# NSA's heads in pairs on halves of the array, a ring of three score banks, and the scalings on Pool

## The chip, the core and the metric

The kernel runs on one core of one Trainium2 chip. The metric is the device time in microseconds; three runs of the kernel before took 2819.25, 2820.51 and 2828.82 us, median 2820.51. Engines: PE (TensorE), DVE (VectorE), ACT (ScalarE), POOL (GpSimd) and SP (SyncE, which issues transfers). Each has its own queue of instructions, in order; they meet through semaphores.

## The reference

One step of a decoder layer on 320 tokens: 256 of a prompt and 8 sequences of 8 new tokens, each with 256 past tokens. A SwiGLU, then a token mixing of two kinds of heads, then a second SwiGLU, each with a layer norm. The change touches only the token mixing. Cut to what matters:

```
# GLA, 4 heads (dk 128, dv 256), per chunk of 64 tokens; b = cumsum(log_a)
attn = einsum('bhik,bhijk,bhjk->bhij', qi, exp(b_i - b_j, causal), ki)
o    = einsum('bhij,bhjv->bhiv', attn, vi) + einsum('bhik,bhkv->bhiv', qi * exp(b), S)
S    = exp(b_last) * S + einsum('bhjk,bhjv->bhkv', ki * exp(b_last - b), vi)
o_g  = head_rms_norm(o_g, gla_norm_g) * silu(gr)

# NSA, 16 heads of 64 on 4 key/value heads: three softmaxes over the same queries,
o_c = cmp_attention(q, k_cmp, v_cmp)     # compressed keys, 15 of them
o_s = sel_attention(q, ...)              # selected blocks
o_w = window_attention(q, ...)           # a window of 512
o_n = g[..., 0:1] * o_c + g[..., 1:2] * o_s + g[..., 2:3] * o_w    # g: three gates per head
```

All is float32. With 256 past tokens the selected blocks cover everything, so the selected and the window branch are two causal softmaxes over the same positions with different keys and values.

## The kernel before

The program is a row of stages: first SwiGLU, projection, mixing, output projection, second SwiGLU. `mixing_stage` is written by hand: one block of instructions for each engine, with semaphores between them. After a preparation it runs a loop of slots, and the order in which each engine's block goes through a slot is the order of its queue.

*NSA.* There are 40 items: 32 heads (two key/value groups `p`, a half `a` = 0 or 1, a query `g`, and a query tile `qt` whose keys are 128 or 256 wide) and the eight sequences, put in at items 9, 13, ... 37. For item i: PE's `scores` (L1218 main, L1222 compressed; L1233, L1234, L1236 for a sequence), DVE's `item` (causal mask L1441, maxima L1453 and L1465, bias L1467), ACT's `exps` (L1637, L1639, with row sums), DVE's weights in the next slot (reciprocal L1450, gate L1463) and the three scalings of the probabilities (L1472 to L1474), PE's `turn` (transposes, L1260 and L1264), ACT's `take` (L1653, L1658), PE's `outputs` (L1277, L1279; L1289, L1291 for a sequence) and ACT's `out`. A head uses 64 rows of the array for scores (`a` chooses which) and 64 columns for outputs. The turn of an item stands LAG = 3 slots behind its scores, the outputs 4; the probabilities have a ring of four buffers, scores alternate between banks 0 and 1, outputs between 4 and 5. The past keys of a sequence are turned by `turn_keys` (L1245) and taken by ACT (L1646).

*GLA.* Eight levels, each of them also the state step of one sequence. A level takes two slots: in the first PE makes its scores (L1141, L1135) and DVE merges them (L1375); in the second PE makes the inter product (L1150) and the state product of a sequence (L1157), DVE makes the differences (L1350, L1351), the next level's q (L1357) and the state (L1384). ACT makes the decay (L1586), the keys of one sequence (`k_one`, L1591) and copies the inter bank (L1610); POOL the next level's k (L1524) and the gate's products with the norm's weights (L1553). GLA's jobs alternate between banks 6 and 7 in the order of `gjobs`: a job may start when the one before last on that list has been read.

PE's order in a slot: keys to turn, scores of item i, turn of item i-3, outputs of item i-4, GLA.

Of the kernel before, what the change touches and what calls it, by code (L numbers as in the profile page):

```python
# [34 lines left out]
P = 128  # L35
# [35 lines left out]
def constants():  # L71
# [32 lines left out]
    for b in range(NB):  # L104
        c[b * TS:(b + 1) * TS, K_SEQ + b] = 1.0
    return c
# [720 lines left out]
def mixing_stage(L, s):  # L827
# [3 lines left out]

    nc, A, O, bank, proj = L.nc, L.A, L.O, L.bank, L.proj
# [14 lines left out]
    k_tok = L.sb("k_tok", [P, 3, GH * P], scope=s)  # L847
# [4 lines left out]
    k_one = [L.sb(f"k_one{i}", [NS, GH * P], scope=s) for i in range(2)]  # L852
# [12 lines left out]
    S_cmp = [L.sb(f"scores_cmp{i}", [P, 16], scope=s) for i in range(2)]  # L865
    PR = L.sb("probs", [P, RING, 2 * GW + 16], scope=s)
    PT = [L.sb(f"probs_turned{i}", [P, 5, P], scope=s) for i in range(2)]
    stat = [L.sb(f"stat{i}", [P, 5, 3], scope=s) for i in range(RING)]
    k_cmp = L.sb("k_cmp", [P, NB + 1, 2, 16], scope=s)
    v_small = L.sb("v_small", [48, NB + 1, 256], scope=s)  # L870
# [8 lines left out]
    R = PR[:].rearrange("p i w -> p (i w)")[:, 0:2 * KV * P].rearrange("p (n k m) -> p n k m", n=2, k=KV)  # L879
    xc, xs = (x[:].rearrange("p a b -> p (a b)").rearrange("p (i t) -> p i t", i=2) for x in PT)  # L880
# [11 lines left out]
    items = [(p, a, g, qt) for qt in range(2) for p in range(2) for g in range(G) for a in range(2)]  # L892
    FIRST, EVERY = 9, 4
    for b in range(NB):
        items.insert(FIRST + EVERY * b, None)
    seq = {FIRST + EVERY * b: b for b in range(NB)}
    at_item = {b: i for i, b in seq.items()}
    NI = len(items)
    SLOTS = NI + LAG + 1
    turns = []  # L900
    for i in range(SLOTS):
        for n in range(2):
            if i + 2 - n in seq:
                turns.append(("k", seq[i + 2 - n], n))
        if LAG <= i < NI + LAG:
            turns.append(("p", i - LAG, 0))
    turn_no = {x: n for n, x in enumerate(turns)}

# [7 lines left out]
    for step in range(1, 2 * LEVELS + 1):  # L916
        if step % 2:
            gjobs += [("score", (step + 1) // 2, j) for j in range(parts((step + 1) // 2))]
        else:
            gjobs += [("inter", step // 2 - 1), ("state", step // 2 - 1, 0), ("state", step // 2 - 1, 1)]  # L920
    O_STEP = 2 * LEVELS + 1
    P_STEP, MS_STEP = O_STEP + 4, O_STEP + 5
# [7 lines left out]
    def last_score(lv):  # L930
# [3 lines left out]
    diffed, made_e, made_q, made_k, q_in, k_made, squared, rooted, o_step, o_inverse = (  # L934
        L.sem("gla_" + x) for x in ("diff", "e", "q", "k", "q_in", "k_one", "squared", "root", "o_step",
                                    "o_inverse"))
# [12 lines left out]
    scored, masked, maxed, exped, summed, weighed, turned, taken, small_taken, out_ready, out_taken = (  # L949
        L.sem("att_" + x) for x in ("scored", "masked", "maxed", "exped", "summed", "weighed", "turned",  # L950
                                    "taken", "small_taken", "out_ready", "out_taken"))

    def width(i):
        return GW if i in seq else (items[i][3] + 1) * P
# [17 lines left out]
    with nc.Block() as block:  # L972
        @block.sync
        def _(sp):
# [52 lines left out]
            for i in range(SLOTS):  # L1027
                if i >= 3 and i % 2 and (i - 3) // 2 < NB:
                    store_state((i - 3) // 2)
                if i >= 4 and i % 2 == 0 and 2 <= i // 2 < NB:  # L1030
                    load_state(i // 2)
                if i == 5:
                    sp.wait_ge(kv_stored, 16 * (6 + 2 + NB))
                    sp.wait_ge(cleared, 3)
# [10 lines left out]
                if i in seq and seq[i] + 2 < NB:  # L1045
                    b = seq[i] + 2
                    sp.wait_ge(turned, turn_no["k", b - 2, 1] + 1)
                    past(b, 0, past_k[b % 2], k_in[b % 2])
                if i - LAG - 2 in seq and seq[i - LAG - 2] + NV < NB:
                    b = seq[i - LAG - 2] + NV  # L1050
                    sp.wait_ge(out_ready, at_item[b - NV] + 1)
                    past(b, 1, past_v[b % NV], v_in[b % NV])
                if i == P_STEP + 1:
# [4 lines left out]
                if i == MS_STEP + 2:  # L1058
# [9 lines left out]
        def _(pe):  # L1068
# [76 lines left out]
            def gla_state(b):  # L1145
# [28 lines left out]
            def gla_step(g):  # L1174
                if g == 0:
# [7 lines left out]
                    gla_scores(0)  # L1183
                elif g < O_STEP and g % 2:
                    gla_scores((g + 1) // 2)
                elif g < O_STEP:
                    gla_state(g // 2 - 1)
                elif g < P_STEP:
                    for n in (2 * (g - O_STEP), 2 * (g - O_STEP) + 1):
                        gla_output(n)  # L1190
                elif g == P_STEP:
# [7 lines left out]
                elif g < MS_STEP + 2:  # L1199
                    for h in (2 * (g - MS_STEP), 2 * (g - MS_STEP) + 1):  # L1200
# [7 lines left out]
            def scores(i):  # L1208
                if i >= 2:
                    pe.wait_ge(exped, 3 * (i - 1))  # L1210
                main, small = bank[i % 2], bank[2]
                if i not in seq:
                    p, a, g, qt = items[i]
                    w = width(i)
                    r = slice(a * HD, (a + 1) * HD)
                    qT = proj[r, T_NQ + 4 * p + g, qt * P:(qt + 1) * P]
                    for n in range(2):
                        pe.matmul(main[:, n * w:(n + 1) * w], qT, proj[r, T_KV + 4 + 4 * n + p, 0:w],  # L1218
                                  start=True, stop=True)
                    if i:  # L1220
                        pe.wait_ge(masked, 2 * i)
                    pe.matmul(small[:, 32:48], qT, k_cmp[r, NB, p], start=True, stop=True).then_inc(scored, 1)  # L1222
                    return
                b = seq[i]
# [3 lines left out]
                c = TP + b * TS  # L1228
                for p in range(2):
                    o = slice(64 * p, 64 * p + 64)  # L1230
                    qT = q_s[:, p, b].rearrange("p a c -> p (a c)")
                    for n in range(2):
                        pe.matmul(main[o, n * 256:(n + 1) * 256], qT, KT[b % 2][:, n, p], start=True, stop=True)  # L1233
                        pe.matmul(small[o, 16 * n:16 * n + 16], qT, proj[:, T_KV + 4 + 4 * n + p, c - TS:c + TS],  # L1234
                                  start=True, stop=True)
                    mm = pe.matmul(small[o, 32:48], qT, k_cmp[:, b, p], start=True, stop=True)  # L1236
# [12 lines left out]
            def turn(i):  # L1249
                if turn_no["p", i, 0]:  # L1250
                    pe.wait_ge(taken, turn_no["p", i, 0])
                pe.wait_ge(weighed, i + 1)
                if i >= 2:
                    pe.wait_ge(out_taken, i - 1)
                w, x = PR[:, i % RING], bank[4 + i % 2]
                chunks = min(width(i), PAST) // P
                for n in range(2):
                    at = WIN + 16 if n and i in seq else n * WIN
                    for g in range(chunks):
                        pe.transpose(bank[3][:, (chunks * n + g) * P:(chunks * n + g + 1) * P],  # L1260
                                     w[:, at + g * P:at + (g + 1) * P], ident)
                if i in seq:
                    pe.transpose(x[0:32, 2 * P:3 * P], w[:, NEW:NEW + 32], ident)
                pe.transpose(x[0:16, P:2 * P], w[:, CMP:CMP + 16], ident).then_inc(turned, 1)  # L1264

            def outputs(i):
                pe.wait_ge(small_taken, i + 1)
                pt, x = PT[i % 2], bank[4 + i % 2]
                if i not in seq:
                    p, a, g, qt = items[i]  # L1270
                    kv = 2 * p + a
                    o = x[a * HD:(a + 1) * HD, 0:P]
                    chunks = width(i) // P
                    for n in range(2):
                        for c in range(chunks):
                            at = (3 + 2 * n) * 256 + kv * HD
                            pe.matmul(o, L.kv_tok[:, c, at:at + HD], pt[:, chunks * n + c],  # L1277
                                      start=(n == 0 and c == 0), stop=False)
# [589 lines left out]
```

## Time and profile before

| | |
|---|---|
| median of three runs | 2820.51 us |
| profiled execution | 2824.61 us |
| its span in the profile | 2822.4 us |
| mean granted clock of PE | 0.958 |
| PE busy in the span | 2718.7 us, 96% |
| DVE, ACT, POOL busy | 1563.6, 460.6, 762.9 us |

What is predicted is the median; the parts are read from the one profiled execution. A row of windows gives for a stretch of the span the busy time of each engine and, as PEclk, the mean clock that PE was granted, as a share of its upper level of 2.4 GHz; 0.5 is the lower level. The mixing's loop of slots lies between 1425.4 and 1684.3 us.

### The profile page before, as it was taken

Reading aid. Unit: us, or ns where it says so; the run is one execution under the profiler, and the core shown is the slowest. Engines: PE = TensorE matmul, PEld = TensorE weight load, DVE = VectorE, ACT = ScalarE, POOL = GpSimd, SP = SyncE. Lnnn points to the kernel's source line nnn. Section 1 sums busy time; section 2 is a strip of 40 time slices with the busy share of each in tenths; the row PEclk is TensorE's granted clock in tenths of the full one; section 3 lists DMA queues with packets and bytes.
Section 4 is the critical chain, followed back from the end, with each engine's and each line's share of the span. In section 5 each row is a group of like instructions: output and inputs, shape, how many; then the busy total and the mean of one; then the engine's idle time right before and its main releaser. Section 6 shows DMA issues by size and latency. Waiting matters only on the chain. (4 is left out here: it accounts for less than half of the span.)

```text
span 2822.4 us, 45319 instructions
## 1 busy us (share of the span) xinstructions
PE 2718.7 (96%) x17691; PEld 2606.0 (92%) x17691; DVE 1563.6 (55%) x1539; ACT 460.6 (16%) x1106; POOL 762.9 (27%) x564
## 2 busy tenths in 40 slices
PE   8999999999999999999799989899999999999997
PEld 7999999899999979999477769789999999999996
DVE  5555556455555665554355565565565565565555
ACT  2110001111000140000344560131100000000002
POOL 1331332133133630000211034443223313323352
PEclk9999999999999999999777999989999999999998
DMA  6555555455555435674322316435455455555552
GB/s 185 149 154 159 149 148 145 129 149 158 157 149 149 133 97 154 180 149 119 119 91 75 104 42 147 111 105 149 134 164 149 136 162 149 140 143 163 149 138 78
DMA packets 735573, 384.97 MB, mean 136 GB/s; under 512 B 65546, under 2 KB 729994, under 8 KB 735194
## 3 DMA queue, kind: packets, MB, share of 16 engines
q1 hardware_dynamic: 735386, 384.17, 49.7%
q8 instruction: 32, 0.52, 0.1%
q14 instruction: 27, 0.22, 0.0%
q10 hardware_dynamic: 128, 0.05, 0.0%
HBM read 372.24 MB, written 16.00 MB: 138 GB/s over the span
## 5 line engine op out<-in xcount | busy, mean ns | idle before, releaser
L316 PE MATMUL bank<-xh_before,wh_before 128*128 128x320 f32 x2112 | 657.6, 311 | 14.0 <-DVE wl_before L334 13.9
L317 PE MATMUL bank<-xl_before,wh_before 128*128 128x320 f32 x2112 | 656.1, 311 | 0.0
L318 PE MATMUL bank<-xh_before,wl_before 128*128 128x320 f32 x2112 | 655.8, 311 | 0.0
L316 PE MATMUL bank<-xh_after,wh_after 128*128 128x320 f32 x1664 | 521.4, 313 | 23.7 <-DVE wl_after L334 15.2
L332 DVE CAST wh_before<-raw 128x2048 fp32r<-128x2048 f32 (+1 forms) x196 | 219.9, 1122 | 579.8 <-PE bank L318 537.6
L317 PE MATMUL bank<-xl_after,wh_after 128*128 128x320 f32 x1664 | 518.4, 312 | 0.0
L318 PE MATMUL bank<-xh_after,wl_after 128*128 128x320 f32 x1664 | 518.3, 311 | 0.0
L334 DVE TENSOR_TENSOR wl_before<-raw,wh_before 128x2048 fp32r<-128x2048 f32 (+1 forms) x196 | 463.5, 2365 | 6.7
L332 DVE CAST wh_after<-raw 128x2048 fp32r<-128x2048 f32 (+1 forms) x168 | 184.9, 1101 | 437.2 <-PE bank L318 435.3
L316 PEld LDWEIGHTS bank<-xh_before,wh_before 128*128 128x128 f32 x2112 | 399.6, 189 | 15.8 <-issue 12.3
L334 DVE TENSOR_TENSOR wl_after<-raw,wh_after 128x2048 fp32r<-128x2048 f32 (+1 forms) x168 | 409.5, 2438 | 5.8
L317 PEld LDWEIGHTS bank<-xl_before,wh_before 128*128 128x128 f32 x2112 | 399.5, 189 | 0.4 <-issue 0.4
L318 PEld LDWEIGHTS bank<-xh_before,wl_before 128*128 128x128 f32 x2112 | 399.6, 189 | 0.0
L552 POOL TENSOR_TENSOR proj<-proj 128x320 f32<-128x320 f32 x88 | 126.5, 1438 | 893.8 <-ACT proj L537 893.8
L316 PEld LDWEIGHTS bank<-xh_after,wh_after 128*128 128x128 f32 x1664 | 315.5, 190 | 29.5 <-DVE wl_after L334 15.8
L317 PEld LDWEIGHTS bank<-xl_after,wh_after 128*128 128x128 f32 x1664 | 316.3, 190 | 0.0
L318 PEld LDWEIGHTS bank<-xh_after,wl_after 128*128 128x128 f32 x1664 | 316.1, 190 | 0.0
L316 PE MATMUL bank<-ffn_hh,wh_after 128*128 128x320 f32 x704 | 217.9, 310 | 0.9 <-POOL ffn_hl L557 0.9
L316 PE MATMUL bank<-ffn_hh,wh_before 128*128 128x320 f32 x704 | 217.9, 309 | 0.0
L318 PE MATMUL bank<-ffn_hh,wl_before 128*128 128x320 f32 x704 | 217.5, 309 | 0.0
L317 PE MATMUL bank<-ffn_hl,wh_after 128*128 128x320 f32 x704 | 217.5, 309 | 0.0
L317 PE MATMUL bank<-ffn_hl,wh_before 128*128 128x320 f32 x704 | 217.5, 309 | 0.0
(239 smaller groups left out, 3253.2 us busy)
## 6 DMA issues: line engine op xcount, KB each, us to landing
raw<-in_w_ffn_in SPq DMA_DIRECT2D x176, 1024.0 KB, 5.6
raw<-in_w_ffn_out SPq DMA_DIRECT2D x128, 704.0 KB, 4.9
raw<-in_w_in SPq DMA_DIRECT2D x36, 1024.0 KB, 5.5
raw<-in_w_in SPq DMA_DIRECT2D x16, 512.0 KB, 5.2
raw<-in_w_out SPq DMA_DIRECT2D x16, 512.0 KB, 4.4
raw<-in_w_out SPq DMA_DIRECT2D x64, 128.0 KB, 4.2
proj<-in_cache_cmp_kv SPq DMA_DIRECT2D x64, 64.0 KB, 2.4
raw<-in_state_gla SPq DMA_DIRECT2D x8, 512.0 KB, 3.5
```

What stands on the lines that cost most here:

```text
L316: pe.matmul(out, L.wh[a][:, w], hi[:, k], start=(k == 0), stop=False)
L317: pe.matmul(out, L.wh[a][:, w], lo[:, k], start=False, stop=False)
L318: last = pe.matmul(out, L.wl[a][:, w], hi[:, k], start=False, stop=(k == nk - 1))
L332: dve.tensor_copy(L.wh[a][:, 0:n], L.raw[a][:, 0:n]).then_inc(L.hi[a], 1)
L334: dve.tensor_tensor(L.wl[a][:, 0:n], L.raw[a][:, 0:n], L.wh[a][:, 0:n].bitcast(F32), ALU.subtract).then_inc(L.split[a], 1)
L552: pool.tensor_tensor(hid, gate, up, ALU.mult).then_inc(product, 1)
```

## The change

*Units.* The 40 items become 24 units: eight pairs (`a` = 0 and 1 together) of width 128, then eight times a sequence and a pair of width 256. There are 25 slots; a unit's turn and outputs stand one slot behind its scores, and the probabilities have a ring of two units. A GLA level takes one slot.

*Halves.* The score matmuls of a pair alternate between `a` = 0 and 1, that is between rows 0 to 63 and 64 to 127, each head into a bank of its own out of a ring of three (0, 1, 5); both compressed scores are one matmul with `k_pair`. The output matmuls alternate between the two halves of the columns, into bank 4 alone. GLA's state products alternate between row halves as well: `k_new` and `k_one` hold two heads' keys in each half of the partitions, and the new tokens' values stand in both halves.

*Orders.* DVE: `maxima` of unit i, GLA's step, `weights` of unit i. ACT: first take of unit i-1, exps of unit i, second take, GLA's step, first key take, out, second key take. PE: scores of unit i, first turn of unit i-1, GLA's scores, second turn, inter and state, keys, outputs of unit i-1, keys.

*Pool.* The scalings of the probabilities go from DVE to POOL (`scale`), six for a pair. The Newton steps of GLA's norm go from POOL to DVE, as four operations over all heads; its products stay on POOL, in later slots.

```
-    LAG, NV = 3, 2
-    RING = LAG + 1
+    NV, RING = 2, 2
...
+    units = [("pair", p, g, 0) for p in range(2) for g in range(G)]
+    for n in range(8):
+        units += [("seq", n), ("pair", n // G, n % G, 1)]
+    ring, ring_at, last_user, frees = (0, 1, 5), {}, {}, {}
...
-                for j in range(2):
-                    to, made = claim(("state", b, j))
-                    for h in (2 * j, 2 * j + 1):
-                        mm = pe.matmul(to[:, h % 2 * DV:(h % 2 + 1) * DV], k_one[b % 2][:, h * P:(h + 1) * P],
-                                       v_gla[0:NS, 2, h * DV:(h + 1) * DV], start=True, stop=True)
-                    mm.then_inc(made, 1)
+                to = [claim(("state", b, j)) for j in range(2)]
+                for h in range(2):
+                    for j in range(2):
+                        r = slice(j * NS, (j + 1) * NS)
+                        mm = pe.matmul(to[j][0][:, h * DV:(h + 1) * DV], k_one[b % 2][r, h * P:(h + 1) * P],
+                                       v_gla[r, 2, (2 * j + h) * DV:(2 * j + h + 1) * DV], start=True, stop=True)
...
+                    for n in range(2):
+                        for a in range(2):
+                            r = slice(a * HD, (a + 1) * HD)
+                            pe.matmul(main(i, a)[:, n], proj[r, T_NQ + 4 * p + g, qt * P:(qt + 1) * P],
+                                      proj[r, T_KV + 4 + 4 * n + p, 0:w], start=True, stop=True)
...
             for i in range(SLOTS):
-                if i <= NI:
-                    item(i)
+                if i < NU:
+                    maxima(i)
                 gla_step(i)
+                if i < NU:
+                    weights(i)
...
+            def scale(i):
+                st, wd = stat[i % RING], width(i)
+                pool.wait_ge(summed, 3 * i + 3)
+                for a in range(heads(i)):
+                    w = PR[:, i % RING, a]
+                    pool.tensor_scalar(w[:, 0:wd], w[:, 0:wd], st[:, 3, a, 1:2], None, ALU.mult)
+                    pool.tensor_scalar(w[:, WIN:WIN + wd], w[:, WIN:WIN + wd], st[:, 3, a, 2:3], None, ALU.mult)
+                    pool.tensor_scalar(w[:, CMP:CMP + 16], w[:, CMP:CMP + 16], st[:, 3, a, 0:1], None, ALU.mult
+                                       ).then_inc(weighed, 1)
```

How the orders stand in the queues, at three places. In such a row the number behind L is the line, then the operation, out<-in, the tile, and in brackets the semaphores it waits for.

ACT before, from the exps of a head on in the slot of a state step (L1586 decay, L1591 k_one, L1681 queries, L1646 key take, L1653 and L1658 take, L1666 out, L1637 next exps); the copy of the inter bank, L1610, is three rows further on, in the next slot:

```order
L1639 ACTIVATE probs,stat<-scores_cmp,stat 128x16
L1586 ACTIVATE proj<-proj 128x4x256 [waits gla_diff]
L1591 ACTIVATE k_one<-k_tok,cst 64x512 [waits gla_bank_made1]
L1681 ACTIVATE proj<-proj 64x8x8 x4
L1646 ACTIVATE raw<-bank 128x512 [waits att_turned]
L1653 ACTIVATE probs_turned<-bank 128x256 [waits att_out_ready,att_turned]
L1658 ACTIVATE probs_turned<-bank 16x128
L1666 ACTIVATE proj<-bank 64x128 [waits att_out_ready]
L1637 ACTIVATE probs,stat<-bank,stat 128x128 [waits att_turned,att_maxed]
```

ACT now, a whole slot of a level (L1715 and L1727 take, L1697 and L1699 exps of both heads, L1642 decay, L1647 k_one, L1668 inter copy, L1735 out):

```order
L1715 ACTIVATE probs_turned<-bank 128x2x256 [waits att_out_ready,att_turned]
L1727 ACTIVATE probs_turned<-bank 16x2x128
L1697 ACTIVATE probs,stat<-bank,stat 128x128 [waits att_turned,att_biased_max]
L1697 ACTIVATE probs,stat<-bank,stat 128x128
L1699 ACTIVATE probs,stat<-scores_cmp,stat 128x16
L1697 ACTIVATE probs,stat<-bank,stat 128x128 x2
L1699 ACTIVATE probs,stat<-scores_cmp,stat 128x16
L1642 ACTIVATE proj<-proj 128x4x256 [waits gla_diff]
L1647 ACTIVATE k_one<-k_new,cst 128x256 [waits gla_bank_made1]
L1668 ACTIVATE inter<-bank 128x8x8 [waits gla_bank_made0]
L1735 ACTIVATE proj<-bank 128x128 [waits att_out_ready]
```

The inter copy, which freed its bank in another slot than the decay, stands behind the decay and k_one of its own slot. PE before, the slot of a state step from its turn on (L1260 and L1264 turn, L1277 and L1279 outputs, L1150 inter, L1157 state):

```order
L1260 MATMUL bank<-cst,probs 128x128 [waits att_out_taken,att_weighed,att_taken]
L1260 MATMUL bank<-cst,probs 128x128
L1264 MATMUL bank<-cst,probs 16x128
L1277 MATMUL bank<-probs_turned,kv_tok 64x128 [waits att_small_taken]
L1277 MATMUL bank<-probs_turned,kv_tok 64x128
L1279 MATMUL bank<-probs_turned,v_small 64x128
L1150 MATMUL bank<-q_samples,raw 128x8 [waits gla_bank_free0,gla_q_in,state_in1]
L1150 MATMUL bank<-q_samples,raw 128x8 x7
L1157 MATMUL bank<-v_gla,k_one 128x256 [waits gla_bank_free1,gla_k_one]
L1157 MATMUL bank<-v_gla,k_one 128x256
L1157 MATMUL bank<-v_gla,k_one 128x256 [waits gla_bank_free0]
L1157 MATMUL bank<-v_gla,k_one 128x256
```

PE now, the slot of a level from the turn of the second head on (L1292 and L1297 turn; the row ahead of these waits for att_weighed; L1166 and L1160 the level's scores, L1175 inter, L1183 state):

```order
L1292 MATMUL bank<-cst,probs 128x128
L1297 MATMUL bank<-cst,probs 16x128 [waits att_out_taken]
L1297 MATMUL bank<-cst,probs 16x128
L1166 MATMUL bank<-xT 128x128 [waits gla_bank_free0,gla_k,gla_q]
L1166 MATMUL bank<-xT 128x128 x3
L1166 MATMUL bank<-xT 128x128 [waits gla_bank_free1]
L1166 MATMUL bank<-xT 128x128 x3
L1160 MATMUL bank<-xT 64x64 [waits gla_bank_free0]
L1160 MATMUL bank<-xT 64x64 x3
L1175 MATMUL bank<-q_samples,raw 128x8 [waits gla_bank_free1,gla_q_in,state_in1]
L1175 MATMUL bank<-q_samples,raw 128x8 x7
L1183 MATMUL bank<-v_gla,k_one 128x256 [waits gla_bank_free1,gla_bank_free0,gla_k_one]
```

A level's scores and its state stand in one slot, and the first state product waits for both banks. POOL before, at the first levels (L1524 k of the next level, L1553 the products with the norm's weights):

```order
L1524 TENSOR_TENSOR xT<-proj 128x640 [waits gla_bank_made0,gla_e]
L1549 MEMSET proj 128x1024 [waits tokens]
L1553 TENSOR_SCALAR proj<-proj,norm_g 128x320 [waits cmp_acted]
L1524 TENSOR_TENSOR xT<-proj 128x320x2 [waits gla_bank_made0,gla_e]
L1553 TENSOR_SCALAR proj<-proj,norm_g 128x320
```

POOL now, at the same place (L1571 k, L1608 the norm's weights, L1579 to L1581 the scalings):

```order
L1571 TENSOR_TENSOR xT<-proj 128x640 [waits gla_bank_made0,gla_e]
L1608 TENSOR_SCALAR proj<-proj,norm_g 128x320 [waits cmp_acted]
L1579 TENSOR_SCALAR probs<-probs,stat 128x128 [waits att_summed]
L1580 TENSOR_SCALAR probs<-probs,stat 128x128
L1581 TENSOR_SCALAR probs<-probs,stat 128x16
L1579 TENSOR_SCALAR probs<-probs,stat 128x128
L1580 TENSOR_SCALAR probs<-probs,stat 128x128
L1581 TENSOR_SCALAR probs<-probs,stat 128x16
```

The six scalings of a unit stand behind the next level's k and one product with the norm's weights.

## Rows read from the trace of the kernel before

**Rows 1.** Windows: stretch, length, busy PE, PEld, DVE, ACT, POOL; PEclk, DMA share, GB/s.
```profile
1425.40:1684.30 258.90, 249.87 (x1476) 199.81 (x1476) 159.03 (x555) 129.57 (x462) 46.34 (x49) 0.83 0.21 67
1434.80:1551.10 116.30, 115.32 (x619) 93.17 (x618) 72.38 (x247) 51.20 (x187) 17.17 (x14) 0.71 0.24 75
1610.00:1640.00 30.00, 27.73 (x149) 21.37 (x148) 25.24 (x69) 16.50 (x62) 16.17 (x22) 0.77 0.15 45
1608.60:1615.40 6.80, 4.94 (x30) 3.64 (x29) 5.07 (x15) 5.34 (x18) 1.50 (x2) 0.91 0.27 77
1615.40:1618.80 3.40, 3.40 (x14) 2.41 (x13) 3.37 (x11) 1.73 (x8) 0.22 (x1) 0.50 0.00 0
```
**Rows 2.** Busy by line, PE, 1425.4 to 1684.3: busy us, mean ns, idle before.
```profile
L1218 PE MATMUL bank<-proj 64*128 64x128 f32 (+1 forms) x128 | 33.3, 387 | 0.6 <-issue 0.6
L1277 PE MATMUL bank<-probs_turned,kv_tok 128*64 128x128 f32 x192 | 32.8, 315 | 0.0
...
L1157 PE MATMUL bank<-v_gla,k_one 64*128 64x256 f32 x64 | 25.1, 557 | 0.0
```
**Rows 3.** Timeline of PE in the GLA levels: start, us, line, tile, shape, count.
```profile
1434.81 2.05 PE L1141 MATMUL bank<-xT 128*128 128x128 f32 x16
...
1443.68 0.63 PE L1157 MATMUL bank<-v_gla,k_one 64*128 64x256 f32 x1
1443.85 0.63 PE L1218 MATMUL bank<-proj 64*128 64x128 f32 x2
...
1459.08 3.78 PE L1141 MATMUL bank<-xT 128*128 128x128 f32 x16
...
1485.41 1.99 PE L1157 MATMUL bank<-v_gla,k_one 64*128 64x256 f32 x8
```
**Rows 4.** Busy by line and shape, DVE and ACT, 1425.4 to 1684.3.
```profile
L1384 DVE SCALAR_TENSOR_TENSOR raw<-raw,decay_samples,bank 128x256 f32<-128x256 f32 x32 | 13.9, 477 | 15.7 <-PE bank L1157 15.6
...
L1375 DVE COPY_PREDICATED xT<-lvl,bank 128x512 f32<-128x512 uint8 x16 | 11.4, 728 | 14.5 <-PE bank L1141 14.4
...
L1472 DVE TENSOR_SCALAR probs<-probs,stat 128x256 f32<-128x256 f32 x16 | 7.2, 451 | 0.0
...
L1450 DVE RECIPROCAL stat<-stat 128x3 f32<-128x3 f32 x40 | 7.0, 176 | 0.0
...
L1591 ACT ACTIVATE k_one<-k_tok,cst 64x512 f32<-64x512 f32 x8 | 5.7, 711 | 0.0
...
L1586 ACT ACTIVATE proj<-proj 128x1024 f32<-128x1024 f32 x5 | 5.2, 1044 | 0.0
...
L1472 DVE TENSOR_SCALAR probs<-probs,stat 128x128 f32<-128x128 f32 x16 | 4.6, 289 | 0.0
...
L1350 DVE TENSOR_TENSOR proj<-xT 128x512 f32<-128x512 f32 x5 | 3.4, 684 | 0.0
...
L1610 ACT ACTIVATE inter<-bank 128x64 f32<-128x64 f32 x8 | 1.8, 220 | 4.1 <-PE bank L1150 4.1
```
**Rows 5.** POOL, one line each: xcount, duration ns min/median/max, first and last start.
```profile
L1553 POOL TENSOR_SCALAR proj<-proj,norm_g x8: 1071/1082/1112, 1432.9 to 1526.9; 128x320 f32<-128x320 f32 x8
...
L1557 POOL TENSOR_SCALAR proj<-proj x4: 458/472/491, 1629.6 to 1630.9; 128x320 f32<-128x320 f32 x4
```
**Rows 6.** Timeline of one 256-wide head late in the loop, PE, ACT, DVE.
```profile
1652.76 1.13 PE L1218 MATMUL bank<-proj 64*128 64x256 f32 x4
1652.81 0.47 ACT L1637 ACTIVATE probs<-bank,stat 128x256 f32<-128x256 f32 x1 [0.18 <-DVE stat L1467]
...
1654.05 0.43 DVE L1441 TENSOR_TENSOR bank<-bank,cst 128x256 f32<-128x256 f32 x1 [0.59 <-PE bank L1222]
...
1654.66 0.66 PE L1260 MATMUL bank<-cst,probs 128*128 128x128 f32 x4 [0.65 <-ACT raw L1646]
1654.68 0.67 DVE L1453 TENSOR_REDUCE stat<-bank 128x2 f32<-128x512 f32 x1
...
1655.46 0.60 ACT L1653 ACTIVATE probs_turned<-bank 128x512 f32<-128x512 f32 x1 [0.85 <-PE bank L1264]
```

More of the change, by code:

```diff
@@ L889, in mixing_stage, with seq, heads, width @@
     NJ, EARLY = len(tjobs), 12
[L892 to L899, printed above, removed]
+    units = [("pair", p, g, 0) for p in range(2) for g in range(G)]
+    for n in range(8):
+        units += [("seq", n), ("pair", n // G, n % G, 1)]
+    NU = len(units)
+    at_unit = {x[1]: i for i, x in enumerate(units) if x[0] == "seq"}
+    SLOTS = NU + 1
+    def seq(i):
+        return units[i][1] if 0 <= i < NU and units[i][0] == "seq" else None
+    def heads(i):
+        return 1 if units[i][0] == "seq" else 2
+    def width(i):
+        return GW if units[i][0] == "seq" else (units[i][3] + 1) * P
+    def goes(i):
+        return 2 if units[i][0] == "pair" and units[i][3] else 1
     turns = []
     for i in range(SLOTS):
[L902 to L906, printed above, removed]
-    turn_no = {x: n for n, x in enumerate(turns)}
+        if i >= 1:
+            turns += [("p", i - 1, n) for n in range(goes(i - 1))]
+        if seq(i + 1) is not None:
+            turns += [("k", seq(i + 1), n) for n in range(2)]
+    turn_no = {x: n for n, x in enumerate(turns)}
+    exp_no = [0]
+    for i in range(NU):
+        exp_no.append(exp_no[-1] + 3 * heads(i))
+    ring, ring_at, last_user, frees = (0, 1, 5), {}, {}, {}
+    for i in range(NU):
+        for a in range(heads(i)):
+            r = ring[len(ring_at) % len(ring)]
+            ring_at[i, a], frees[i, a] = r, last_user.get(r, 0)
+            last_user[r] = exp_no[i] + 3 * a + 2
+    def main(i, a):
+        w = min(width(i), PAST)
+        return bank[ring_at[i, a]][:, 0:2 * w].rearrange("p (n k) -> p n k", n=2)
     LAST = LEVELS
@@ L915, in mixing_stage @@
     gjobs = [("turn", t) for t in range(3)] + [("score", 0, j) for j in range(3)]
[L916 to L922, printed above, removed]
+    for step in range(1, LEVELS + 1):
+        gjobs += [("score", step, j) for j in range(parts(step))]
+        gjobs += [("inter", step - 1), ("state", step - 1, 0), ("state", step - 1, 1)]
+    O_STEP, MS_STEP = LEVELS + 1, LEVELS + 4
     gjobs += [("o", n) for n in range(2 * GH)] + [("final", i) for i in range(2)] + [("ms", h) for h in range(GH)]
@@ L1266, in outputs @@
             def outputs(i):
                 pe.wait_ge(small_taken, i + 1)
[L1268 to L1272, printed above, removed]
+                x = bank[4]
+                if seq(i) is None:
+                    _, p, g, qt = units[i]
                     chunks = width(i) // P
@@ L1503, in _ @@
             dve.wait_ge(k_ready, 1)
-            dve.wait_ge(cleared, 3)
+            dve.wait_ge(cleared, 4)
+            rows = bank[0][:, 0:NQ * 2 * NC].rearrange("p (b k n) -> p b k n", b=NQ, k=2)
+            for a in range(2):
+                r = slice(a * HD, (a + 1) * HD)
+                dve.tensor_copy(k_pair[r, :, a, 0:NC], rows[r, NB])
             dve.tensor_copy(k_cmp[:, :, :, 0:NC],
@@ L1579, in take_tokens @@
                     to = v_gla if what == "v" else L.kv_tok
+                    if what == "v" and t == 2 and n == 1:
+                        act.activation(v_gla[NS:P, 2, 512:1024], b[0:rows, :], ACT.Copy)
                     act.activation(to[0:rows, t, n * 512:(n + 1) * 512], b[0:rows, :], ACT.Copy
@@ new lines, in take @@
+                if go < goes(i) - 1:
+                    return
+                x = bank[4]
+                if seq(i) is not None:
+                    act.activation(PT[0:32, 0, 4], x[0:32, 2 * P:3 * P], ACT.Copy)
+                    act.activation(PT[32:48, 0, 4], x[0:16, P:2 * P], ACT.Copy).then_inc(small_taken, 1)
+                else:
+                    act.activation(PT[32:48, :, 4], x[0:16, P:3 * P].rearrange("p (a k) -> p a k", a=2), ACT.Copy
+                                   ).then_inc(small_taken, 1)
```

502 lines of the change are left out of this document (260 added, 242 removed).

## The prediction

> **What bounds the kernel now.** I read the stage windows first, then what ends PE's idle time in the one stage that the change touches, then that stage's timeline. The loop over heads, sequences and GLA levels runs from 1425.4 to 1684.3: 258.9 us, in which PE is busy 249.87 at a granted clock of 0.83 [rows 1]. Nothing else comes near: DVE 159, ACT 130, POOL 46. So PE bounds the loop, and it is bounded by a PE that runs slowly: 249.87 × 0.83 = 207 us of work at the full 2.4 GHz. The reader is to see two things. The lag of three items and the ring of four buffers keep PE supplied whatever a single head waits for: in the 116.3 us of the levels PE is idle for 1 us. And the clock is not held by a full PE alone: in those 116.3 us it is 0.71 [rows 1]. Outside the loop only a few small copies change; I hold the rest of the program fixed.
>
> The rows say what the lower clock costs: the two large parts of a level's scores take 2.05 us at the upper level and 3.78 at the lower [rows 3]. They also say what can bring a fall: in the 6.8 us from 1608.6 PE was busy for 4.94 (73%), and the 3.4 us behind it ran at 0.50 [rows 1].
>
> **The change part by part.**
>
> *Halves of the array.* L1218 (33.3 us), L1277 (32.8) and L1157 (25.1) are the matmuls that use half of the rows or columns [rows 2]; after the change they stand in pairs on different halves. That they overlap is seen already where L1157 and L1218 happen to alternate: one starts 0.17 us after the other, each lasting 0.63 [rows 3]. At best 91.2 us become 45.6, at worst nothing is saved. I take the half: 45.6 × 0.83 = 38 us of full-clock work, which leaves 207 − 38 = 169.
>
> *Slack.* The lag falls from three items to one unit, the ring of probabilities from four heads to two units, and one level takes one slot instead of two. What is cut from PE's work is worth something only if PE still has work while a unit waits. I therefore add up the chain that comes round once per slot.
>
> *A level slot* (eight, 128-wide pairs; PE terms at the upper clock). DVE's `weights` come behind the whole GLA step now, three small operations on one another: 0.5 (0.176 each, [rows 4]). Then POOL scales both heads: 2.6, below. PE's turn of the second head, behind POOL: 0.45 (four such transposes are 0.66, [rows 6], and two small ones). The level's two large parts behind it in PE's queue: 2.05 [rows 3]. DVE's merge of the last, 0.73; q of the next level, 0.68; the two differences, 1.37 [rows 4]. ACT's decay, which waits for the differences, 1.04; `k_one`, 0.4 (half of 0.711); and the copy of the inter bank, 0.22 [rows 4]. In before that copy is not behind a decay, and the first half of the state doesn't need its bank; now both state banks are claimed at once, and one of them is the bank that this copy frees. Then the state matmuls in halves, 1.0 (1.99, [rows 3]), the four DVE updates, 1.9 (0.477 each, [rows 4]), and ten handovers at about 0.08. Sum: 13.8. What is queued behind the waits: on PE the outputs of the last pair, on DVE the weights of this one, for which POOL and then PE wait.
>
> *POOL's scalings.* The trace has no 128-wide one. The same operation with a scalar per partition on POOL is L1553: 1.08 us for 320 columns [rows 5]. In proportion 128 columns are 0.43, the lower bound; 1.08, if width didn't matter, the upper. L1557, with constants, takes 0.47 for 320, and would give 0.19. On DVE the operation goes from 0.289 to 0.451 between 128 and 256 columns, so that 0.13 of it is fixed [rows 4]. I take 0.43 + 0.13 = 0.56, nearest to the row of the same form: 4 × 0.56 + 2 × 0.18 = 2.6 per pair of 128. If every large one took 1.08 it would be 4.7, and 17 us more over eight levels; by L1557 1.6, and 8 less.
>
> The Trainium skill, "GPSIMD Engine Reference", section 4.1 (Engine selection), puts elementwise work on VectorE and calls one-input work on GPSIMD roughly line-rate. By that rule 128 columns would cost about DVE's 0.289 and the pair 1.5, and the forecast would fall by 9 us to 2852. L1553 doesn't bear that out: 1.08 for 320 against DVE's 0.451 for 256 [rows 4, 5].
>
> *A late cycle* (eight: one sequence and one 256-wide pair). Exps of three heads, 3.6 (two of 0.47 and a small one each, [rows 6]); ACT's take of a pair, 0.87, and of the keys, twice 0.6 [rows 6]; PE's turn of keys between them, 0.6; outputs of the pair 1.4; its scores 1.25 (two heads in the 1.13 of one, [rows 6]); its maxima 2.3 (0.43 and 0.67 twice and the small ones, [rows 6]); scores and maxima of the sequence, 1.5 and 1.75, estimates from the same rows; thirteen handovers at 0.1. Sum: 15.8. The scalings hide here: POOL's 2.2 per 256-wide head (in proportion, with the same 0.13 each) and 2.3 per sequence run beside the next unit's scores, maxima and exps.
>
> *The rest.* Until the first weights, 12. GLA's outputs, roots and reciprocals in the middle slots, which now stand between maxima and weights, 16 beyond what the cycles cover. POOL's norm steps go to DVE as four wide operations: inside those 16, and 3 to 6 more if the cover fails. The two `k_pair` copies, its memset and one more ACT copy lie ahead of the loop beside loads: nothing, at most 1.
>
> *Sum at the upper clock:* 12 + 8 × 13.8 + 8 × 15.8 + 16 = 264. *At the lower:* PE's 169 becomes 338, and it is then PE that fills most of a slot; the waits that no order fills (the start, and some 2 us in each late cycle) add 27: 365. Between them I go by 264 + 101 × (1/clock − 1).
>
> **Which clock.** At the upper level PE would be busy for 169 of 264 us, 64%. The only stretch of the loop with so little was the 73% ahead of a fall [rows 1]. At the lower level it is busy for 338 of 365, as in the levels of before. I expect it to go up and down, and take what before had in the nearest stretches: 0.71 in the levels, 0.77 from 1610 to 1640, where a sequence, heads and GLA's norm meet [rows 1]. Mean 0.74: 264 + 101 × 0.351 = 299.5, which is 40.6 more than 258.9. The profiled execution took 2824.61 (span 2822.4 and 2.2 around it); with 40.6 it is 2865.2. It lies 4.1 above the median of the runs, 2820.51, so the forecast for the median is 2861.
>
> **The rivals.**
>
> *The clock stays up (A).* For it: the loop of before had 0.83 on the whole and 0.91 in the very stretch of 73%, and work that alternates between halves might be denser than the busy share tells. Against it: the 73% row, and 64% here. At 1.0 the loop is 264: 2826; with the cheap POOL scalings 256: 2818; at 0.9 275: 2837. Not slower, then, by what can be measured. To be faster the late cycle would have to shrink as well, by letting the maxima and exps of a sequence hide behind the pair's matmuls (15.8 − 3 = 12.8, so 240 and 2802). The point that decides: a granted clock in the loop above 0.9.
>
> *The clock stays down (B).* For it: waits recur in every slot, and the levels of before had 0.71 with hardly a wait. Against it: at the lower level PE is almost full. At 0.55 the loop is 347: 2908; all of it at the lower level 365: 2926.
>
> *The halves don't overlap (C),* so that the change doesn't do what it says. For it: a pair's matmuls load different weights each time, and L1157 beside L1218 shows two lines of work, not eight in a row. Against it: those rows. Each level is 1.0 longer, each late cycle 2.6: 293 at the upper level, 414 + 27 = 441 at the lower, 345 at 0.74: 2907.
>
> **How the numbers follow.** The forecast (slower, 2838 to 2890, POOL's upper bound in it at 2878) has 0.55, A 0.22, B 0.14, C 0.09. About 0.5% of this kernel, 14 us, is what a measurement can tell from no change: 2806 to 2835 is the same. From A comes 0.07 for faster and some 0.13 for the same; the forecast's lower edge gives 0.03 more, 0.16 in all; slower has 0.77. The range reaches into A at its low end and to B and C at its high end: 2814 to 2912. The forecast's own is 2838 to 2890.
>
> **What would show it.** In the windows of the profile after: a loop of about 300 us with PE busy clearly under 90% of it and a mean clock between 0.65 and 0.85; ahead of PE's turns, idle time ended by POOL's scalings in the levels; DVE's state updates waiting for PE, PE's state waiting for ACT's inter copy, and that copy starting right behind the decay. The first 128-wide scalings on POOL near 0.56. Two scores of a pair that start within 0.1 us of one another. In a late cycle, PE idle until ACT's takes. I would be wrong if PE were busy throughout (then the chain is not what bounds it), if a level slot took under 12 us at the upper clock, or if the loop's clock were above 0.9.

## The result and the profile after

Four runs of the changed kernel took 2869.58 to 2878.84 us, median 2872.79, beside 2819.88 for the kernel before: ratio 1.0183, 95% interval [1.0156, 1.021]. It is slower by 53 us, where 41 were forecast. The profiled execution has a span of 2872.0 us, 49.6 more than before, and the loop of slots accounts for all of it: 1421.67 to 1735.73, 314.1 us in place of 258.9. It starts 3.8 us earlier, and what follows is 1.8 us shorter. (The profiled execution is one run, 1 us above the median here and up to 10 us beside it in the experiments; the ratios go by all runs.) Windows of the profile after (columns as in [rows 1]): the loop, six level slots, five late cycles.

```profile
1421.70:1735.70 314.00, 242.29 (x1444) 191.02 (x1444) 126.57 (x343) 118.40 (x422) 119.50 (x153) 0.66 0.18 56
1436.30:1537.00 100.70, 75.93 (x424) 61.23 (x426) 47.40 (x117) 32.98 (x125) 42.62 (x49) 0.60 0.17 49
1621.80:1725.90 104.10, 77.24 (x459) 57.17 (x459) 41.62 (x108) 45.79 (x161) 46.07 (x61) 0.63 0.12 36
```

PE is busy for 242.3 of 314 us (77%, before 97%) at a clock of 0.66 (before 0.83): 160 us of work at the upper clock, before 207. So the pairing saved 47 us of PE's work, and the loop is 55 us longer. What PE waits for, from the waits of the profile after (us in total, times, longest):

```profile
PE bank L1292 <- POOL probs L1581: 21.1, 22, 3.8
PE bank L1183 <- ACT inter L1668: 16.2, 8, 3.1
PE bank L1312 <- ACT probs_turned L1727: 9.2, 6, 2.7
```

One level slot in order of time, from the timeline after (start, us, engine, line, count, idle before and what ended it):

```profile
1469.42 0.17 DVE L1516 TENSOR_TENSOR stat<-stat,gate_tok 128x6 f32<-128x6 f32 x1
1469.67 0.60 POOL L1579 TENSOR_SCALAR probs<-probs,stat 128x128 f32<-128x128 f32 x1 [3.62 <-DVE stat L1516]
...
1472.29 0.33 POOL L1581 TENSOR_SCALAR probs<-probs,stat 128x16 f32<-128x16 f32 x1
...
1472.67 0.69 PE L1292 MATMUL bank<-cst,probs 128*128 128x128 f32 x2 [0.70 <-POOL probs L1581]
...
1473.58 3.62 PE L1166 MATMUL bank<-xT 128*128 128x128 f32 x16
...
1477.23 0.73 DVE L1417 COPY_PREDICATED xT<-lvl,bank 128x512 f32<-128x512 uint8 x1 [0.98 <-PE bank L1166]
...
1478.04 3.22 POOL L1571 TENSOR_TENSOR xT<-proj 128x512 f32<-128x512 f32 x1 [5.42 <-PE bank L1160]
...
1479.46 0.68 DVE L1393 TENSOR_TENSOR proj<-xT 128x512 f32<-128x512 f32 x1
1480.17 1.06 ACT L1642 ACTIVATE proj<-proj 128x1024 f32<-128x1024 f32 x1 [3.26 <-DVE proj L1393]
...
1481.53 0.20 ACT L1668 ACTIVATE inter<-bank 128x64 f32<-128x64 f32 x1
...
1481.88 2.08 PE L1183 MATMUL bank<-v_gla,k_one 64*128 64x256 f32 x8 [1.85 <-ACT inter L1668]
...
1483.96 1.66 DVE L1426 SCALAR_TENSOR_TENSOR raw<-raw,decay_samples,bank 128x256 f32<-128x256 f32 x4 [3.82 <-PE bank L1183]
...
1485.96 0.17 DVE L1516 TENSOR_TENSOR stat<-stat,gate_tok 128x6 f32<-128x6 f32 x1
```

The reader is to see a relay: apart from POOL's L1571, which stands beside the chain, and DVE's q and first difference, which are not shown ahead of L1393, each row starts where the one ahead of it ends, and the round closes after 16.5 us with the same operation. POOL's six scalings of a unit stand between DVE's weights and PE's turn; the inter copy is behind the decay and `k_one`, and PE's state behind the copy.

### The profile page after: what moved, and what is told of

It reads as the page before. It is cut to its first block and busy times, and to the rows that moved or that the text cites. A ratio compares the mean times of both kernels' runs of the same rounds, so it can differ in the third digit from the quotient of the medians.

```text
span 2872.0 us, 45080 instructions
## 1 busy us (share of the span) xinstructions
PE 2707.6 (94%) x17659; PEld 2593.5 (90%) x17659; DVE 1531.0 (53%) x1329; ACT 450.1 (16%) x1068; POOL 835.0 (29%) x669
## 5 line engine op out<-in xcount | busy, mean ns | idle before, releaser
L319 PE MATMUL bank<-ffn_hh,wl_after 128*128 128x320 f32 x704 | 217.5, 309 | 0.0
```

What stands on the lines that cost most here:

```text
L319: last = pe.matmul(out, L.wl[a][:, w], hi[:, k], start=False, stop=(k == nk - 1))
```

## The experiments

Twelve kernels were run, each timed against the kernel before on the chip that it ran on. The loop and its clock are those of the profiled execution.

| kernel | loop us | clock | PE busy us | ratio to before, 95% |
|---|---|---|---|---|
| before | 258.9 | 0.83 | 249.9 | 1 |
| changed | 314.1 | 0.66 | 242.3 | 1.0183 [1.0156, 1.021] |
| e1 inter copy first | 305.0 | 0.64 | 249.8 | 1.0133 [1.0102, 1.0164] |
| e2 weights ahead of state | 306.2 | 0.67 | 241.9 | 1.0137 [1.0104, 1.0169] |
| e3 both | 293.1 | 0.69 | 236.0 | 1.0087 [1.0065, 1.0108] |
| e4 scalings on DVE | 290.2 | 0.70 | 230.3 | 1.0109 [1.0089, 1.0128] |
| e5 heads apart | 331.6 | 0.65 | 269.0 | 1.0247 [1.0225, 1.0268] |
| e6 128-wide filler | 291.7 | 0.93 | 240.1 | 1.0093 [1.0071, 1.0115] |
| e7 lag of two units | 282.7 | 0.72 | 222.2 | 1.0111 [1.0077, 1.0145] |
| e8 lag and both orders | 296.5 | 0.67 | 237.0 | 1.014 [1.011, 1.0171] |
| e9 lag, copy first, filler | 296.0 | 0.78 | 248.4 | 1.0069 [1.0048, 1.0091] |
| e10 before with filler | 280.0 | 0.90 | 272.1 | 1.0069 [1.0042, 1.0096] |
| e11 8-wide filler | 392.5 | 0.58 | 354.5 | 1.0447 [1.042, 1.0474] |
| e12 orders, DVE, filler | 291.4 | 0.83 | 242.4 | 1.0095 [1.0077, 1.0113] |

**The chain: e1, e2, e3.** In e1 ACT's block of a level has the inter copy first:

```diff
+                if 1 <= g <= NB:  # the inter copy, moved up
                 if g + 2 <= LAST:
                     decay(g + 2)
                 if 1 <= g < NB:
                     one_sequence(g)
-                if 1 <= g <= NB:  # the inter copy
```

> One edit to the changed kernel: ACT copies the inter bank ahead of the decay and of k_one in each level's slot. Theory (one serial chain per slot sets the loop): PE's state products no longer wait for the decay; in the profile after they wait 1.9 us for that copy in each of eight levels, so the loop falls by about 1.6 us a level, 314 to about 301, and the ratio to the kernel before from 1.018 to about 1.014; PE's idle time ahead of the state falls from 16 us to under 4. Rival (the loop is long because PE runs at 0.66 and is full at that clock): no change, 1.018, and the time saved ahead of the state comes back as waiting elsewhere.

Measured 1.0133; PE's waits for the copy, from the waits of e1, fell from 16.2 to 3.2 us:

```profile
PE bank L1292 <- POOL probs L1581: 20.6, 20, 3.8
...
PE bank L1183 <- ACT inter L1664: 3.2, 8, 0.4
```

The wait for POOL stayed. In e2 DVE's step calls the weights ahead of the state:

```diff
                     if g + 2 <= LAST:
                         difference(g + 2)
+                    weights(g)
                     if g:
                         state(g - 1)
```

> One edit to the changed kernel: DVE makes a unit's weights ahead of the state updates (from level 8 on ahead of GLA's step), not behind them. Theory of the chain: POOL's scalings then run beside PE's state products and DVE's updates; they start when POOL's other two operations are done, about 3.6 us earlier, and PE's turns no longer wait for POOL in the levels. Of the 3.6 some 1.5 to 2 come through, since PE's own scores and outputs stand between: loop 314 to about 300, ratio about 1.013. Rival (POOL's durations, not where they stand, are the cost): under 3 us.

Measured 1.0137; now the wait for POOL falls, from 21.1 to 7.6 us, and that for the copy stays (waits of e2):

```profile
PE bank L1183 <- ACT inter L1669: 14.8, 8, 3.5
...
PE bank L1292 <- POOL probs L1582: 7.6, 5, 3.8
```

e3 has both edits.

> Both edits of order at once: the inter copy ahead of the decay, and the weights ahead of the state updates. Theory of the chain: the gains add, since the one shortens the state's wait and the other takes POOL out of what follows; about 14 + 13 us, less what PE itself then needs: a level 16.8 to about 13.5 us, loop 314 to about 288, ratio 1.009. Rival (each moved the same slack): no better than the better of the two, 1.013.

Measured 1.0087: the gains (0.0050 and 0.0046) add, to within the 0.003 or so by which each ratio is known. Both places are links of the chain; neither is slack.

**POOL: e4.** The body of `scale` moves to DVE, behind the weights:

```diff
                 dve.tensor_tensor(st[:, 3, 0:nh], st[:, 4, 0:nh], gt, ALU.mult).then_inc(summed, 1)
+                scale(i)   # now with dve.tensor_scalar
```

> One part undone: the scalings of the probabilities are on DVE again, right behind the weights, all else as in the changed kernel. Theory of the chain: six on POOL take 2.9 us from the first to the last in a level, on DVE about 1.5, and none of the next maxima is held up for long: 1.3 us a level and about 1 in each late cycle, 18 us in all, ratio about 1.012. Rival (the move to POOL is what made the kernel slower): back to 1.00 or below. Second rival (DVE's queue becomes the chain, the next maxima wait): 1.018 or more.

Measured 1.0109, as the theory had it: PE's wait for the scalings falls from 21.1 to 5.5 us, the one for the copy stays (17.0), and the move to POOL is two fifths of the loss (0.0074 of 0.0183), not all of it.

**The halves: e5.** The same matmuls, with the loop over the heads outside:

```diff
-                    for n in range(2):
-                        for a in range(2):
+                    for a in range(2):
+                        for n in range(2):
```

> One part undone: the same matmuls of a pair, but one head after the other, both in scores and in outputs, and the state's and a sequence's two halves likewise one after the other; banks, waits and everything else as in the changed kernel. Theory (halves overlap when alternated): a level is about 1.7 us longer at the lower clock by the state alone and about as much by scores and outputs, a late cycle by 2.6 to 4 us: loop up by 25 to 45 us, ratio 1.027 to 1.034. Rival (the halves don't overlap, so that alternating brings nothing): 1.018.

Measured 1.0247, a little under the theory's range. Two late outputs of the changed kernel, then of e5, from PE's timelines, both at the lower clock:

```profile
1715.24 1.97 PE L1312 MATMUL bank<-probs_turned,kv_tok 128*64 128x128 f32 x16 [1.11 <-ACT probs_turned L1727]
1717.14 0.69 PE L1316 MATMUL bank<-probs_turned,v_small 16*64 16x128 f32 x4
1717.77 2.08 PE L1247 MATMUL bank<-proj 64*128 64x256 f32 x8
```

```profile
1705.16 1.97 PE L1312 MATMUL bank<-probs_turned,kv_tok 128*64 128x128 f32 x8 [2.35 <-ACT probs_turned L1726]
1707.06 0.69 PE L1315 MATMUL bank<-probs_turned,v_small 16*64 16x128 f32 x2
1707.67 1.97 PE L1312 MATMUL bank<-probs_turned,kv_tok 128*64 128x128 f32 x8
1709.57 0.68 PE L1315 MATMUL bank<-probs_turned,v_small 16*64 16x128 f32 x2
1710.19 2.09 PE L1247 MATMUL bank<-proj 64*128 64x256 f32 x8
```

Alternated, sixteen records of outputs take as long as eight of one head: the column halves overlap fully. The scores take 2.08 and 2.09 us in either order, about half of what two heads one after the other would take at this clock (2 × 1.13 at the upper, [rows 6]): with two matmuls in a row on each row half, the order makes no difference. The same holds of the state. Busy by line of the changed kernel, outputs and state, then of e5:

```profile
L1312 PE MATMUL bank<-probs_turned,kv_tok 128*64 128x128 f32 x192 | 22.1, 393 | 9.2 <-ACT probs_turned L1727 9.2
L1183 PE MATMUL bank<-v_gla,k_one 64*128 64x256 f32 x64 | 14.7, 600 | 16.2 <-ACT inter L1668 16.2
```

```profile
L1312 PE MATMUL bank<-probs_turned,kv_tok 128*64 128x128 f32 x192 | 45.4, 402 | 8.8 <-ACT probs_turned L1726 8.8
L1183 PE MATMUL bank<-v_gla,k_one 64*128 64x256 f32 x64 | 15.3, 619 | 17.1 <-ACT inter L1667 17.1
```

So e5 took the overlap from the outputs alone, which is why it cost less than expected: the expectation counted on 1.7 us a level from the state.

**The slack: e7, e8.** In e7 a unit's turn and outputs stand two slots behind its scores, with a ring of three units:

```diff
-    NV, RING = 2, 2
+    NV, RING = 2, 3
-    SLOTS = NU + 1
+    LAG = 2
+    SLOTS = NU + LAG
-                if i >= 1:
-                    turn(i - 1, 0)
+                if i >= LAG:
+                    turn(i - LAG, 0)
```

> Slack given back: the turn and the outputs of a unit stand two slots behind its scores and the probabilities have a ring of three units; the orders within a slot, POOL's scalings and the halves stay as in the changed kernel. Theory (the lost lag is what costs): weights, POOL and the turn leave the chain; a level 10.7 us at the upper clock and a late cycle about as long as PE's own work, 12; with one more slot 222 us at the upper clock and some 275 at a clock of about 0.7: ratio about 1.006. Rival (POOL's scalings bound it wherever they stand): under 10 us better than the changed kernel, 1.015.

PE no longer waits for POOL ahead of a turn, as the theory had it, and the kernel is 20 us faster than the changed one, which is not the rival's outcome. The loop of the profiled execution is 282.7, near the 275 expected, but that was the fastest of four runs from 2846 to 2866, and the ratio is 1.0111, not 1.006. e8 adds the orders of e3.

> Lag of two units and both edits of order. Theory: as with the lag alone and 1.6 us less in each level, so that PE is nearly full; about 210 us at the upper clock, 255 to 265 at 0.72 or so: ratio 0.998 to 1.003. If the clock rises to the 0.83 of the kernel before, about 240 and 0.993. Rival (the clock is lower wherever matmuls are paired on halves): clock at or under 0.66 with PE full, loop above 275, ratio above 1.006.

Measured 1.014, worse than e3 alone: the rival's time and nearly its clock, though PE is not full (busy for 80%). The profiled loop has PE's full-clock work unchanged (237.0 × 0.67 = 159), less waiting for the copy than e7 (3.2 against 11.3 us), about as much idle time of PE in all (59.5 and 60.5 us), and a lower clock, 0.67 against 0.72. Moving the waits did not bring the clock; whether the pairing lowers it, as the rival has it, is not shown.

**The clock: e6, e10, e11.** e6 adds matmuls whose results are overwritten, at two places where PE waits:

```diff
+                for _ in range(8 if go == 0 else 0):      # in turn, ahead of the wait for POOL
+                    pe.matmul(bank[3][:, 0:P], ident, ident, start=True, stop=True)
...
+                for _ in range(6):                        # ahead of the state products
+                    pe.matmul(to[0][0][:, 0:P], ident, ident, start=True, stop=True)
```

> The changed kernel with work added that nobody reads: eight transposes' worth of 128x128 matmuls ahead of each turn's wait for POOL and six ahead of each state's wait for k_one, in banks that are overwritten afterwards (0.92 and 0.69 us each at the upper clock, twice that at the lower; 29 us in all at the upper). They stand where PE waits. Theory (the clock falls because PE waits): PE's busy share rises from 77% to about 88%, the granted clock from 0.66 to 0.75 or more, and the loop is no longer than 314 us though PE does more, perhaps 10 to 15 shorter: ratio 1.012 to 1.019. Rival (the clock has nothing to do with these waits): clock 0.66 as before, and what of the fillers doesn't fit into the waits is added, 10 to 25 us: ratio 1.022 to 1.027.

Each of them takes 0.25 us at the upper clock (two records in the trace), not the 0.115 I had reckoned with: they add some 63 us of work, twice what the expectation says. The kernel became faster than the changed one all the same, 1.0093, below the range of the theory, with PE busy for 82% and not the 88% expected. Windows of e6, its first part, the rest, and the whole loop:

```profile
1424.72:1550.00 125.28, 104.03 (x868) 89.79 (x869) 65.98 (x169) 45.66 (x171) 55.17 (x67) 0.95 0.21 63
1550.00:1716.40 166.40, 136.12 (x1059) 112.94 (x1057) 61.77 (x175) 72.09 (x251) 63.52 (x87) 0.92 0.18 57
1424.72:1716.40 291.68, 240.14 (x1924) 202.72 (x1924) 127.75 (x343) 117.75 (x422) 118.68 (x153) 0.93 0.19 59
```

240.14 × 0.93 = 223 us of full-clock work in place of 160, in 22 us less. A level of e6 at the upper clock, PE's timeline, the turn of the second head in two slots, and the added work between:

```profile
1472.40 0.44 PE L1297 MATMUL bank<-cst,probs 128*128 128x128 f32 x2 [1.02 <-POOL probs L1586]
...
1472.90 1.95 PE L1166 MATMUL bank<-xT 128*128 128x128 f32 x16
...
1482.36 2.03 PE L1288 MATMUL bank<-cst 128*128 128x128 f32 x16
...
1485.84 0.44 PE L1297 MATMUL bank<-cst,probs 128*128 128x128 f32 x2 [1.02 <-POOL probs L1586]
```

This one takes 13.44 us from turn to turn; the five levels from 1458.83 to 1527.83, all at a clock of 1.00, take 69.0 us, 13.8 each. PE waits for POOL even behind the filler: this is the chain at the upper clock, forecast at 13.8. e10 puts four such matmuls into every turn of the kernel before, where PE hardly waits.

> The kernel before, with four added 128x128 matmuls that nobody reads in each of the 40 turns, behind their waits and so on PE's path: 18 us at the upper clock, 37 at the lower. Theory A (waits of PE alone lower the clock): PE was full, so the clock stays at 0.83 and the loop is 22 us longer: ratio 1.007 to 1.009. Theory B (what the work consists of counts too: in the levels of before the clock was 0.71 with PE full): the clock rises to 0.93 or more, 207 + 18 = 225 us at the upper clock become 235 to 243, ratio 0.992 to 0.995.

Measured 1.0069, just under theory A's range, but not for its reason. Windows of e10, as for e6:

```profile
1423.15:1550.00 126.85, 123.92 (x771) 104.13 (x772) 76.93 (x256) 53.73 (x196) 20.96 (x17) 0.81 0.23 71
1550.00:1703.10 153.10, 148.22 (x1026) 121.59 (x1025) 84.08 (x299) 75.89 (x266) 25.32 (x32) 0.98 0.17 56
1423.15:1703.10 279.95, 272.14 (x1796) 225.71 (x1796) 161.01 (x555) 129.61 (x461) 46.29 (x49) 0.90 0.20 63
```

The added work is 40 us, and the loop is 21 longer: the clock rose from 0.83 to 0.90, with PE as full as it had been. e11 is e6 with 8 columns in place of 128:

```diff
-                    pe.matmul(bank[3][:, 0:P], ident, ident, start=True, stop=True)
+                    pe.matmul(bank[3][:, 0:8], ident, L.cst[:, K_ID:K_ID + 8], start=True, stop=True)
```

> The changed kernel with as many added matmuls, at the same places, as in the run with fillers (eight ahead of a first turn, six ahead of a state), but 8 columns wide, not 128. One 8-wide matmul takes PE about as long as a 128-wide one (0.24 us against 0.25 at the upper clock, from eight of each in the profiles), so that PE's busy time is the same, some 60 us at the upper clock and not the 29 given before. Theory A (PE's waits set the clock): as with the wide ones, clock 0.9 or more, ratio 1.007 to 1.012. Theory B (what the work consists of sets it, as the levels of the kernel before with PE full at 0.71 suggest): clock no higher than 0.75, loop 320 or more, ratio 1.020 or more.

Measured 1.0447. The loop of e11 in the windows:

```profile
1424.86:1817.40 392.54, 354.53 (x1924) 300.48 (x1924) 124.85 (x343) 118.68 (x422) 118.62 (x153) 0.58 0.14 45
```

PE is busy for 90% of it, more than in the changed kernel (77%) or in e6 (82%), and the granted clock is the lowest of all. So the busy share doesn't tell the clock. What the chip goes by these runs don't settle.

**Combinations: e9, e12.** e9 is e7 with the copy first and about half of the filler; e12 is e3 with the scalings on DVE and a smaller filler. Neither beats the kernel before, whose time lies below both intervals.

> The lag of two units, the inter copy ahead of the decay, and a smaller dose of the added matmuls that nobody reads (four ahead of each first turn, four ahead of each state: 15 us at the upper clock). Theory (what is left of the loss with the longer lag is the clock, and dense work lifts it): granted clock in the loop above 0.85, a level 10.2 us and a late cycle 13.4, loop 235 to 250, ratio 0.990 to 0.997, below the kernel before. Rival (the added work lifted the clock before only because it filled waits, and here there are few): clock about 0.72 as with the longer lag alone, the added work on top of 283 less 10: ratio 1.010 to 1.015.

Measured 1.0069 and a clock of 0.78: between the theory and the rival. The filler is some 32 us of PE time (128 × 0.25), not 15.

> All that helped, at a lag of one unit: the inter copy ahead of the decay, the weights ahead of the state updates, the scalings on DVE behind the weights, and a dose of 128-wide added matmuls (six ahead of a first turn, two ahead of a state: 0.25 us each, 42 us of PE time at the upper clock). Theory (chain and clock together): a level about 10 us and a late cycle about 15 at the upper clock, 228 in all; at a clock of 0.85 to 0.95 some 235 to 250: ratio 0.991 to 0.997. If the clock stays under 0.8, 255 to 265 and 0.999 to 1.002. Rival (the added work stands in PE's path once the waits are gone): above 1.005.

Measured 1.0095 with a clock of 0.83: the rival's outcome. 242.4 × 0.83 = 201 us of full-clock work, 41 of them filler, which now stands in PE's path: a turn waits for the scalings once in the whole loop (1.5 us). A wait that the changed kernel's matmuls did not have shows instead, for the transfer of a sequence's state (waits of e12; 5.6 us in e2, 5.8 in e8):

```profile
PE bank L1175 <- DMA raw<-in_state_gla: 6.1, 5, 2.5
```

## Why the prediction was right, point by point

- *Halves.* Right: 169 us of full-clock work were forecast, 160 measured. For the outputs e5 shows the overlap; the eight records of a state took 1.99 us before [rows 3] and take 2.08 now at half the clock. Matmuls outside the forecast's 91.2 us gained too: a sequence's scores took 21.3 us in all before (L1233), now 13.1 (L1262). Rival C falls.
- *A level slot.* Right: 13.8 at the upper clock, 13.8 in e6 (mean of five); in the changed kernel 16.8 (six in 100.7 us) at a clock of 0.60. In the slot shown, of 16.5, PE's terms took 6.6 in place of 3.5. e1 and e2 each take out one link, and the time falls by about what the link held.
- *POOL's scalings.* 0.56 and 0.18 us were taken for 128 and 16 columns, 0.60 and 0.35 measured; the six take 2.95 in place of 2.6. That 0.56 came so near is in part luck: by the two widths below, 128 more columns cost 0.32, where 0.43 was taken, and the fixed part is 0.28, where 0.13 was taken from DVE. Nor do the scalings hide altogether in the late cycles: of PE's 21.1 us of waiting for them 9.3 fall behind the levels. Lines of the profile after, busy by line and shape:

```profile
L1580 POOL TENSOR_SCALAR probs<-probs,stat 128x256 f32<-128x256 f32 x16 | 14.8, 922 | 0.0
...
L1581 POOL TENSOR_SCALAR probs<-probs,stat 128x16 f32<-128x16 f32 x40 | 13.9, 348 | 0.0
...
L1580 POOL TENSOR_SCALAR probs<-probs,stat 128x128 f32<-128x128 f32 x16 | 9.6, 602 | 0.0
```

- *The Trainium skill* ("GPSIMD Engine Reference", Engine selection: one-input work roughly line-rate): the trace doesn't agree, 0.602 us on POOL for what took DVE 0.289 [rows 4], and 2.95 for the six where the estimate by that rule was 1.5.
- *Sum and clock.* 264 + 101 × (1/clock − 1) gives 316 at the clock that was granted, 0.66; the loop took 314.1. The term that was mis-sized is the clock: 0.74 was taken from two stretches of before, 0.66 came, and that alone takes the sum from 299.5 to 316. The agreement with 314.1 is one of totals. No run separates the other terms: the five late cycles took 20.8 us each at 0.63, none ran at the upper clock with nothing added to it, so that 15.8 is not confirmed, and the first weights came 14.6 us into the loop where 12 were taken. No run undoes the move of the norm's Newton steps to DVE.
- *Why the clock falls.* I said that PE's waits bring it down. That is not shown. Filling the waits with 128-wide work lifted it to 0.93, but with as many 8-wide matmuls in the same places it was 0.58, below the changed kernel's 0.66; e8, with PE idle for 20% in place of 23%, had no better clock (0.67); and e10 raised it where PE hardly waited. Why it falls stays open. Rival A was wrong for this kernel (0.66, not above 0.9); e6 shows that its clock was within reach. B's 0.55 didn't come either.

How the 55 us divide is thus half shown: e3, which changes the order alone, takes 21 us off the profiled loop (clock 0.69), and e6, at 0.93, takes off 22 in spite of 63 us of added work. The two are not independent, so no shares are given.

## What to carry to other kernels

A change that cuts the work of the busiest engine (here from 207 to 160 us) but brings all its neighbours into one slot can turn a bound by that engine's work into a bound by a round trip: add up one round, engine by engine, before counting what is saved. Look in each queue for short copies that release a bank and stand behind a long operation that waits; moving the one here gave back a quarter of the loss. And take PE's time at both clock levels: here a kernel with more work on PE was faster, because the work ran at a higher clock.

## What was not expected of the hardware

A 128x8 and a 128x128 float32 matmul took PE nearly the same time (0.24 and 0.25 us at the upper clock), yet the loops filled with the one and the other ran at 0.58 and 0.93.

POOL's two-input L1571 and DVE's two-input operations cost one another time where they coincide, and it went either way. In the slot shown L1571 took 3.22 us for 512 columns, while DVE's q and differences beside it kept their 0.68. In the three levels behind it L1571 took 1.25 to 1.27, as before the change (1.27), and DVE's q took 1.29 to 1.31 and a difference 0.93; POOL's one-input L1608 took 2.04 in place of 1.08 beside that difference. Timelines of POOL and DVE in the first of these levels:

```profile
1493.89 1.27 POOL L1571 TENSOR_TENSOR xT<-proj 128x512 f32<-128x512 f32 x1 [4.74 <-PE bank L1166]
1494.39 1.31 DVE L1399 TENSOR_TENSOR xT<-proj 128x512 f32<-128x512 f32 x1
1495.14 2.04 POOL L1608 TENSOR_SCALAR proj<-proj,norm_g 128x320 f32<-128x320 f32 x1
...
1496.23 0.93 DVE L1393 TENSOR_TENSOR proj<-xT 128x512 f32<-128x512 f32 x1
```

L1571 itself is off the chain, but q and the differences are on it, and the forecast took 0.68 for each of them: these levels took 17.0 us, the one shown 16.5.
